# A sparse-attention kernel's tail: one weight split earlier, another order of values, turns and copies, no idle transposes

## The reference

```python
proj = x @ w_in                                   # q, k, v and the indexer's iq, ik, iw
q, k, iq, ik = (partial_rotary(...) for ...)      # 16 query heads, 4 key heads of 64
score = sum_h iw[h] * relu(iq[h] @ ik.T) * 64**-0.5    # causal
sel = top_k(score, 64)                            # 64 keys for each query
logits = (q @ k.T) * 64**-0.5, only where selected and causal
p = softmax(logits)
o = p @ v
h = layer_norm(alpha * x + o @ w_o)
```

## Time and profile before

| | |
|---|---|
| median of three runs | 1242.33 us (1241.86 to 1243.48) |
| span of the profiled execution | 1239.5 us |
| the profiled execution's own time | not given beside its span |
| TensorE busy | 1229.5 us (99%) |
| VectorE busy | 853.1 us (69%) |
| ScalarE busy | 589.4 us (48%) |
| GpSimd busy | 94.9 us (8%) |

### The profile page before, as it was taken

How to read it: one execution, slowest core, us unless ns; L and a number is a source line. 1 busy time by engine, 2 the same in 40 slices (tenths; PEclk the granted TensorE clock), 3 DMA queues, 4 the chain that set the end, 5 groups by cost and what they waited for, 6 DMA issues and landing times.

```text
span 1239.5 us, 18755 instructions
## 1 busy us (share of the span) xinstructions
PE 1229.5 (99%) x7999; PEld 1050.9 (85%) x7999; DVE 853.1 (69%) x919; ACT 589.4 (48%) x712; POOL 94.9 (8%) x226
## 2 busy tenths in 40 slices
PE   9999999999999999999999999999999999999998
PEld 8888888888888888888988888888898888888887
DVE  6887776665775776666776676668587666766675
ACT  5774444334754544334654444345472544444434
POOL 5441000001000200000101000001000100000000
PEclk9999999999999999999999999999999999999999
DMA  8425665655633755654615656555564347655642
GB/s 282 170 69 166 209 197 181 199 187 156 221 115 129 266 183 191 202 175 157 222 60 182 216 181 203 180 194 204 180 191 158 103 150 237 200 186 188 200 141 101
DMA packets 127234, 221.03 MB, mean 178 GB/s; under 512 B 7048, under 2 KB 91296, under 8 KB 127152
## 3 DMA queue, kind: packets, MB, share of 16 engines
q1 hardware_dynamic: 124128, 209.83, 51.0%
q0 software_dynamic: 3024, 10.01, 2.6%
HBM read 218.77 MB, written 1.05 MB: 177 GB/s over the span
## 4 chain that ended last, share of the span: by engine, by line
PE 93%; DVE 3%; ACT 2%; DMA 1%; POOL 1%; issue 1%; SPq 0%; POOLq 0%; DVEq 0%
PE ps L794 20%; PE ps L622 18%; PE ps L796 10%; PE ps L599 10%; PE ps L600 10%; PE ps L601 10%; PE ps L762 4%; PE ps L810 2%; PE ps L706 2%; DVE wlo L1870 1%; PE ps L1034 1%; PE ps L981 1%; DMA raw<-in_ffn_w_in 1%; PE ps L1149 1%; ACT whi L1421 1%
## 5 line engine op out<-in xcount | busy, mean ns | idle before, releaser
L1870 DVE TENSOR_TENSOR wlo<-raw,whi 128x2048 fp32r<-128x2048 f32 (+3 forms) x203 | 452.1, 2241 | 174.6 <-ACT whi L1421 173.4
L1421 ACT ACTIVATE whi<-raw 128x2048 fp32r<-128x2048 f32 (+3 forms) x203 | 376.8, 1869 | 73.0 <-DMA raw<-in_hgrn_w_in 21.7
L794 PE MATMUL ps<-xhl,whi 128*128 128x512 f32 x1088 | 271.8, 392 | 0.0
L794 PEld LDWEIGHTS ps<-xhl,whi 128*128 128x128 f32 x1088 | 198.4, 188 | 37.4
L622 PE MATMUL ps<-whi,xhl 128*128 128x512 f32 (+1 forms) x736 | 182.6, 380 | 0.7 <-ACT xhl L1438 0.6
L599 PE MATMUL ps<-whi,hh 128*128 128x512 f32 x432 | 168.8, 391 | 0.0
L600 PE MATMUL ps<-whi,hl 128*128 128x512 f32 x432 | 168.6, 390 | 0.0
L601 PE MATMUL ps<-wlo,hh 128*128 128x512 f32 x432 | 168.1, 389 | 0.0
L796 PEld LDWEIGHTS ps<-xhl,wlo 128*128 128x128 f32 x1088 | 148.4, 190 | 10.6
L622 PEld LDWEIGHTS ps<-whi,xhl 128*128 128x128 f32 x736 | 130.7, 188 | 26.0 <-issue 0.9
L796 PE MATMUL ps<-xhl,wlo 128*128 128x256 f32 x1088 | 151.7, 282 | 0.0
(11 more groups left out here) (342 smaller groups left out, 1354.8 us busy)
## 6 DMA issues: line engine op xcount, KB each, us to landing
raw<-in_ffn_w_in SPq DMA_DIRECT2D x40, 1024.0 KB, 5.1
raw<-in_mlp_w_up SPq DMA_DIRECT2D x32, 1024.0 KB, 5.4
raw<-in_mlp_w_down SPq DMA_DIRECT2D x32, 1024.0 KB, 4.9
raw<-in_ffn_w_down SPq DMA_DIRECT2D x22, 1024.0 KB, 4.8
raw<-in_hgrn_w_in SPq DMA_DIRECT2D x16, 1024.0 KB, 6.0
raw<-in_b_w_in SPq DMA_DIRECT2D x12, 1024.0 KB, 5.6
raw<-in_ple_w_gate SPq DMA_DIRECT2D x8, 1024.0 KB, 6.0
raw<-in_a_w_in SPq DMA_DIRECT2D x6, 1024.0 KB, 5.8
```

Of the source, the lines that this page charges most:

```text
L794: mm(bank(b + f), w[0][:, kk, P * f : P * f + P], xhl[:, kk, :, :].rearrange("p a n -> p (a n)"), start=(kk == 0), stop=False)
L1421: a.activation(whi[:, slot, 0:w], raw[:, slot, 0:w], ACT.Copy).then_inc(s["hi_done"], 1)
L1870: v.tensor_tensor(wlo[:, slot, 0:w], raw[:, slot, 0:w], whi[:, slot, 0:w].bitcast(F32), ALU.subtract).then_inc(s["lo_done"], 1)
```

## The change

Six edits, all in or around the attention's tail:

1. VectorE's split of output chunk 0 is queued ahead of the attention, behind the mask instructions, no longer behind `output(3)`.
2. The values of units 5 and 7 go to bank 3 (`values_bank`). Those of unit 5 then wait for the last logits to be read from it and no longer for `output(3)`; the ten idle transposes are gone.
3. The last unit's probabilities go to banks 0 and 2, since bank 3 is in use.
4. Unit 6's one copy moves from ScalarE to VectorE.
5. On TensorE, the values of unit 6 come ahead of the transposes of unit 7, and tile 0 of `y` is transposed ahead of the values of unit 7.
6. VectorE's order at the end is: copy of unit 5, copy of unit 6, `output(3)`, `output(6)`, copy of unit 7, the subtraction for the turned tile 0, the splits of chunks 1 and 2, `output(7)`, the split of chunk 3. Before: copy of unit 5, `output(3)`, split of chunk 0, copy of unit 7, `output(6)`, split of chunk 1, the subtraction, `output(7)`, the splits of chunks 2 and 3.

```diff
-        def probs_bank(u):
-            return 1 if u % 2 == 0 else (4 if u < len(ATT_UNITS) - 1 else 2)
+        def probs_bank(u, kt=0):
+            if u == len(ATT_UNITS) - 1:
+                return (0, 2)[kt]
+            return 1 if u % 2 == 0 else 4 + kt
+        def values_bank(u):
+            b, g = ATT_UNITS[u]
+            return 3 if b == 1 and g >= 2 else 6 + b
...
                 def values(u):
...
-                    pe.wait_ge(s["probT_act"], u + 1)
-                    if b == 1:
-                        pe.wait_ge(s["probT_dve"], g + 1)
+                    if u < n_units - 2:
+                        pe.wait_ge(s["probT_act"], u + 1)
+                    elif b == 1:
+                        pe.wait_ge(s["probT_act"], u)
+                    if u == n_units - 2:
+                        pe.wait_ge(s["probT_dve"], n_units // 2)
+                    elif b == 1:
+                        pe.wait_ge(s["probT_dve"], g + 1 + (g == 3))
                     if g == 2:
                         if b == 1:
-                            pe.wait_ge(s["logit_read"], n_units - 1)
-                            keep_fed(10, 0)
-                        pe.wait_ge(s["src_ready"], ready(T_DSA, b, 0, True))
+                            pe.wait_ge(s["logit_read"], n_units)
+                        else:
+                            pe.wait_ge(s["src_ready"], ready(T_DSA, b, 0, True))
...
                 for u in range(n_units):
                     if u + 3 < n_units:
                         logits(u + 3)
+                    if u == n_units - 1:
+                        values(u - 1)
                     turn_probs(u)
-                    if u >= 1:
+                    if 1 <= u < n_units - 1:
                         values(u - 1)
+                turn_tile(T_DSA, y, 0)
                 values(n_units - 1)
-                turn_tile(T_DSA, y, 0)
...
# ScalarE
-                    copies(u)
+                    if u != n_units - 2:
+                        copies(u)
...
# VectorE
                 def copies(u):
+                    b = units[u][0]
                     dve.wait_ge(s["probs_turned"], u + 1)
-                    v.tensor_copy(probT[:, u % 2, 512:1024], bank(probs_bank(u) + 1)).then_inc(s["probT_dve"], 1)
+                    v.tensor_copy(probT[:, u % 2, 512 * b : 512 * b + 512], bank(probs_bank(u, b))).then_inc(s["probT_dve"], 1)
...
                     if u + 2 < n_units:
                         prepare(u + 2)
-                    if units[u][0] == 1:
+                    if u == n_units - 1:
+                        output(u - 1)
+                    if units[u][0] == 1 or u == n_units - 2:
                         copies(u)
-                    if u in (4, 5):
-                        output(u - 2)
-                    if u == 5:
-                        until(first["dsa_o"])
-                output(n_units - 2)
-                until(first["dsa_o"] + 1)
+                    if u == 4:
+                        output(2)
+                    if u == n_units - 2:
+                        output(3)
                 turned(T_DSA, 0)
+                until(first["dsa_o"] + 2)
                 output(n_units - 1)
                 until(first["dsa_o"] + 3)
                 turned(T_DSA, 1)
...
+            until(first["dsa_o"])
             attention(ATT_UNITS, lambda b: bias[:, b, :], float(A_HD**-0.5), A_HEADS)
```

More of the change, by code:

```diff
@@ L908, in turn_probs @@
                             src = logit4[u % 4][:, P * nk * PLACE[b][h] + P * kt : P * nk * PLACE[b][h] + P * kt + P]
-                            last = nc.tensor.transpose(ps[:, probs_bank(u) + kt, P * h : P * h + P], src, ident[:, :])
+                            last = nc.tensor.transpose(ps[:, probs_bank(u, kt), P * h : P * h + P], src, ident[:, :])
                     last.then_inc(s["probs_turned"], 1)
@@ L914, in values @@
                     nk = b + 1
-                    pe.wait_ge(s["probT_act"], u + 1)
-                    if b == 1:
-                        pe.wait_ge(s["probT_dve"], g + 1)
+                    if u < n_units - 2:
[6 more added lines that the diff above has]
+                        pe.wait_ge(s["probT_dve"], g + 1 + (g == 3))
                     if g == 2:
                         if b == 1:
-                            pe.wait_ge(s["logit_read"], n_units - 1)
-                            keep_fed(10, 0)
-                        pe.wait_ge(s["src_ready"], ready(T_DSA, b, 0, True))
+                            pe.wait_ge(s["logit_read"], n_units)
+                        else:
+                            pe.wait_ge(s["src_ready"], ready(T_DSA, b, 0, True))
                     for h in range(4):
-                        o = ps[:, 6 + b, 256 * (g % 2) + hd * h : 256 * (g % 2) + hd * h + hd]
+                        o = ps[:, values_bank(u), 256 * (g % 2) + hd * h : 256 * (g % 2) + hd * h + hd]
                         for kt in range(nk):
@@ L2035, in output @@
                     dve.wait_ge(s["att_pv"], u + 1)
-                    v.tensor_tensor(y[:, b, hd * (4 * g - 4) : hd * (4 * g + 4)].rearrange("p (h d) -> p h d", h=8), bank(6 + b).rearrange("p (h d) -> p h d", h=8),
+                    v.tensor_tensor(y[:, b, hd * (4 * g - 4) : hd * (4 * g + 4)].rearrange("p (h d) -> p h d", h=8), bank(values_bank(u)).rearrange("p (h d) -> p h d", h=8),
                                     rinv[:, b, hs].unsqueeze(2).broadcast_to([P, 8, hd]), ALU.mult).then_inc(s["src_ready"], 1)
```

## The result

| | before | after |
|---|---|---|
| median | 1242.36 us (1241.16 to 1244.06) | 1244.88 us (1243.21 to 1248.74) |
| executions | 18 | 18 |
| ratio after/before | | 1.0026 [1.0019, 1.0032] |
| the profiled execution: span, time | 1239.5 us | 1246.5 us, 1248.43 us |

The kernel became slower where I had written +0.1, and lies outside my range: by 2.5 us by the medians (0.20%), by 0.26% or 3.2 us by the ratio, which weighs the long executions too. The eighteen times form three groups: four of 1243.2 to 1243.4, eight of 1244.4 to 1245.8, and six of 1247.6 to 1248.7. The profiled execution is one of the longest, so its own rows hold more than the median's loss.

What follows compares the result with a forecast made beforehand. TensorE's own queue was taken as the bound (last chain 93% TensorE), with VectorE's also full in the attention. Entrance +1.9 us and tail -1.8 gave +0.1, so 1242.4 us; range 1240.4 to 1243.9.

Steps and rivals of the forecast that it cites:

- Entrance, the delay: Before the queries' transposes: the moved split holds GpSimd's last rotation instruction, which ends 1.93 us late, all reaching the tail.
- Tail: End of the attention: the output projection starts 1.97 us earlier, less 0.2 for chunk 1, a gain of 1.8 us.
- 0.2 was to be lost at chunk 1: Output projection: TensorE waits 0.1 to 0.2 us for VectorE's split of weight chunk 1.
- The idle transposes' part: Tail, before unit 5's values: dropping the ten idle transposes takes off 1.28 us; 1.3 was the tail's lower bound.
- The sum: Whole kernel: +1.9 us at the entrance and -1.8 in the tail give +0.1 us, so 1242.4 us.
- the entrance's price: Entrance: 1.9 us taken for the delay, with bounds of nothing and 2.2 us.
- slower: TensorE, idle for some 2.1 us, comes back at its lower clock: Rival at the entrance, near 61.8 us: lower clock after the gap costs 2.5 us, time 1244.9; chance 0.08.
- a stretch that was busy for 3.77 of 5.00 us at full clock: Argument on the clock: in the 5 us from 636 TensorE was busy only 3.77 and the clock stayed 1.00.
- what is won or lost here stays: After the projection: every weight transfer and wait follows TensorE's own progress, so the tail's gain or loss persists.

Runs made afterwards that it cites:

- experiment 1: Kernel before with only VectorE's split of output chunk 0 moved up, idle transposes kept: 1245.33 us against 1242.68, ratio 1.0026.
- 4: Changed kernel with VectorE waiting for GpSimd's last rotation instruction before it begins the split: 1243.20 us, ratio 1.0005.
- experiment 2: Changed kernel with the split of chunk 0 put ahead of the top-64 search: 1241.63 us, ratio 0.9994; run again, 1242.07 us, 0.9995.
- experiment 3: Changed kernel with ten idle transposes put in front of the queries' transposes, filling part of TensorE's gap: 1242.65 us, ratio 1.0000.

## Why the prediction was wrong

**Entrance, the delay right.** The split arrived under the rotation's last but one instruction and held the last: 2.38 us, a delay of 1.93 as forecast. Experiments 1 and 4 show that it was the split, 2 that the same split does no harm where the GpSimd instruction that it holds isn't on the path. The Trainium skill's page "SBUF — State Buffer", section "Who interferes with whom", states that a VectorE instruction with two SBUF inputs contends with a GpSimd instruction that reads SBUF; trace and page agree (0.46 became 2.38).

**Tail, right and a little too low.** I had 1.97, of which 0.2 was to be lost at chunk 1; it gave 2.17, and from the projection's start to chunk 3 only 0.08 more than before passed. The idle transposes' part was the 1.2 to 1.3 I gave it, but only because the other edits go with it.

**The sum, right without the rest.** With its gap filled the changed kernel is at 1242.65, and with 20 waits its executions at a clock of 1.0 are at 1241.2 to 1242.9, against my 1242.4.

**The step that failed** is the entrance's price: the sum took TensorE's wait of 2.1 us as a bare delay of 1.9 and had no term for the clock behind it. I had it as the rival "slower: TensorE, idle for some 2.1 us, comes back at its lower clock", gave it 0.08 and left it out of the range. It happened in four of five profiles with the gap (the changed kernel twice, experiment 1, the changed kernel with 40 waits) and not in the fifth. Behind 1.04 us idle it did not happen in the one profile of experiment 3, behind 2.1 it mostly did. I had argued against it from a stretch that was busy for 3.77 of 5.00 us at full clock; but its idle time is one wait of 1.23 us. It stands in all 18 profiles and the clock never fell behind it, which says nothing of 2.1 us:

```profile
638.71 1.16 PE L1291 MATMUL ps<-buf 128*128 128x128 f32 x8 [1.23 <-DVE buf L2320]
```

Its price was smaller than I had written: 1.5 to 1.6 us in the four profiles, not 2.5, which I had from transposes at the kernel's start. The Trainium skill's page "TensorE: Matmul & The Clock Gate", section "HAM oscillation — how this bites in real kernels", tells of TensorE coming back at its lower clock behind every wait of 3 to 5 us for a DMA. No run here has a wait of that length between TensorE's products; here one of 2.1 us was enough in four profiles of five.

**The second loss is a term that the sum put at nothing.** I costed the ten idle transposes as TensorE's time only, and wrote that what is won or lost here stays. They are also 20 instructions, and with them gone everything behind stands 20 instructions closer to the program's start, so that the blocks in which instructions arrive end elsewhere in the bursts of tiny products. How the loss is made up, by ratios: the tail's 2.17 pays for the split's 1.93 and the 0.2 outside the span. The gap's clock is the difference of the changed kernel with 40 waits (1.0009) and the filled one (1.0000), some 1.1 us as a mean over executions in which it does and doesn't fall. The stops, and the clock that follows the long one, are taken to be what is left between 1.0009 and the 1.0026 and 1.0020 of the changed kernel: 2.1 and 1.4 us. That gives 3.2 and 2.5 us, which are these two ratios. But each ratio has an interval of some 0.0009 to either side, so the two parts are rough, and the last is a remainder and not measured by itself. That my rival's 1244.9 hits the measured median is chance: it had too much for the clock and nothing for the stops.

**Still open.** Shown is that the stop's place moves with the count, and that TensorE goes on a near constant time behind an instruction packet. Why that packet comes late in one execution and not in another (1.16 and 0.45 us at the first place, 2.01 us and none at the second, in the changed kernel's two profiles) stays open, and so does how often a kernel has a stop, the one before too: there is one profile of most, two of the changed kernel and of that of experiment 2. Open is also what the 0.2 us outside the span are.

**A better version.** The changed kernel with the split ahead of the top-64 search and the instruction count shifted (20 waits inside) is the fastest here: 0.9985 [0.9976, 0.9994], 1.9 us below before, nearly the tail's whole 2.17. With 40 and 100 waits it gives 0.9988, without any 0.9994 and 0.9995. The kernels with waits lie below both without, but the intervals overlap; that the shift itself gains something is likely and not shown.

## What to carry to other kernels

A hole in one engine's queue is free only if what is put there doesn't hold up an instruction of another engine on the path: look at what every other engine is in the middle of, not only at the idle time. Where the path then waits some 2 us on TensorE in one piece, count a fall of the clock as likely, and fill part of the hole. And a change in the number of instructions is a change everywhere behind it: follow the position against the old trace to the last layer, and take several executions, before you put an effect down to the edited place.

## What the runs showed of the hardware

- TensorE stands still for 0.20 to 2.07 us in the middle of a burst of 64 tiny products with no semaphore, and goes on 1.3 to 1.6 us behind the end of a 16 KB packet of the instruction queue (19 times in 18 profiles); the place moves by five products for ten instructions.
- A VectorE split of 128x2048 that came up under a GpSimd instruction took 2.55 us instead of 2.29 and held the next GpSimd instruction, which reads SBUF, until its own end (0.46 became 2.38 us).
- A gap in TensorE's work was followed by the 1.2 GHz level in four profiles (2.14 to 2.18 us), at a cost of 1.5 to 1.6 us (in the changed kernel for 3.4 us), and by nothing in a fifth (2.12); 12 of 62 executions with that gap have a mean clock of 1.0. Of three stops of 1.73, 2.01 and 2.07 us the clock fell behind the second alone, and behind 1.04 us, and behind the 1.23 us near 640 us that all 18 profiles have, it stayed.
- Twenty met waits at TensorE's start cost 0.55 us and 84 cost 4.0, 20 and 40 inside the kernel none that the trace shows, and 100 there 1.27 us of standing still.
